# A state-space stage in another order, with its rotation inside two PSUM banks, and a rotary exchange by DMA copies instead of matmuls

## The chip, the core and the metric

One program on one core of a Trainium2 chip. The metric is the device time of one execution in microseconds (us). Four engines compute: TensorE (PE), VectorE (DVE), ScalarE (ACT) and GpSimd (POOL). SyncE (SP) only issues DMAs. Each engine works through its own queue in order, and semaphores carry the dependences between the queues. Matmuls write to eight banks of PSUM (2 KB per partition each); everything else is in SBUF. POOL and DMAs reach SBUF only.

## What is computed

Four layers on 512 tokens with 1024 channels, in fp32: a state-space and a latent-attention layer, each with a feed-forward, and two closing layers with three kinds of attention. The change touches the scan of the first layer and the partial rotary embedding of the closing ones:

```python
def s5_mixer(h, w_in, lam_re, lam_im, log_step, b_re, b_im, c_re, c_im, d_skip, w_glu):
    u = (h @ w_in).reshape(bsz, seq, 64, 16)             # 64 groups of 16 channels, 64 states each
    step = exp(log_step); decay = exp(lr * step)
    a = decay * (cos(li * step) + i sin(li * step))
    b = f(a, lr, li) * (b_re + i b_im)
    x[l] = a * x[l - 1] + b @ u[l]                        # complex, by an associative scan
    y = real(c @ x) + d_skip * u
    z = gelu(y)
    val, gate = split(z @ w_glu); return val * sigmoid(gate)

def _partial_rope(t, cos, sin):                           # closing layers, heads of 64, 16 dims turned
    x1, x2 = t[..., :8], t[..., 8:16]
    r1 = x1 * cos - x2 * sin
    r2 = x2 * cos + x1 * sin
    return concatenate([r1, r2, t[..., 16:]])
```

## The kernel before

**Products.** A product (L1827) is one tile of 128 output channels by 512 tokens: for each of eight slices of 128 input channels three matmuls, high x high, high x low and low x high (wh and wl, xH and xL), so that 24 float32r matmuls give fp32 accuracy. A weight block of 512 KB is loaded by SP into one of four raw buffers; ScalarE copies it to wh (split_high, L579), VectorE subtracts to get wl (split_low, L1093). Both run two blocks ahead of TensorE (ahead), and there are two buffers of wh and wl, so the copy for block n+2 starts when product n ends.

**Front of the state-space stage.** SP loads x, w_in and the parameters. ScalarE makes xH and the squares (two buffers, freed by TensorE through sq_used), VectorE makes xL. Product 0 of w_in is interleaved with the sum of squares, a plain fp32 matmul with ones of two passes for each slice, in bank 7 (L1969 to L1976). VectorE makes, between its xL steps, the powers of a (denominator, input_gain, powers, gained). From the sum ScalarE makes R, the inverse norm. VectorE multiplies each product by R into T (L1282), SP writes it to u_dram and reads it back in another layout (read_u: eight DMAs a quarter, U). POOL makes the rotation tables Er and Ei (E) and, in make_v, the output tables V (VM); VectorE makes the input tables G (make_g, five operations on 1024 columns) and the last part of Ei (last_phases).

**Four quarters.** The 64 groups go through in four quarters q of 16 groups. TensorE: states(q) (L1901) makes the chunk inputs z in banks 1 and 2; from_g (L1875) transposes G, which ScalarE copies to WM; lags (L1886) makes the short-range kernel; turn_z (L1932) turns the finished z back; outputs(q) applies the short-range kernel MS (Toeplitz, L1914) and then the states through V (L1922), into banks 6 and 3, and raises y_ready. VectorE, in each quarter: turn z by E (six operations with the temporaries rotr, roti, rott), zL of the quarter before, two scans (L1334), turn back (six operations into state), s_ready, make_g(q+2), lag0(q+1). lag0 adds the skip term to the lag row and puts it in MS; SP then spreads it by seven copies inside SBUF (mat_shift), after it has waited for the outputs and issued the reads of the next quarter. ScalarE does gelu (zs), WM, zH, the lag weights C2 and rho, the decay rows. Then comes the product with w_glu.

The queues are written out by hand. states(q+1) waits for z_read, given when VectorE has read both banks for the last time, and stands in TensorE's queue behind outputs(q).

**Closing layers.** For each layer eight tiles of q and k are projected (stage qk). ScalarE copies tile n from its bank to qk. rotate(n) on TensorE multiplies that tile with the constant permutation "rotate" into bank 4 or 5: an fp32 matmul of two passes, placed behind product n+1 (rotate(7) in the stage of v). VectorE's rope(n) then does bank x sin, tile x cos and their sum (L1683 to L1685), after the weight split of its turn. Afterwards POOL fills cq_exact and ck_exact by sixteen small DMAs (L561).

## Time and profile before

| | us |
|---|---|
| median of 3 runs | 1966.43 |
| lowest, highest | 1961.60, 1966.61 |
| the profiled execution | 1966.65 |
| its span in the trace | 1964.9 |
| TensorE busy in it | 1858.9 |
| VectorE, ScalarE, POOL busy | 1069.4, 832.9, 130.7 |

All stretches and rows are of the profiled execution; times count from the start of its span. A row of a timeline gives the start, the duration, the engine, the line of the kernel, the operation with what it writes and reads, and in brackets how long the engine had been idle before and who ended that. x with a number merges consecutive instructions. PEclk, in a stretch, is the granted clock of TensorE as a share of 2.4 GHz; 0.50 is 1.2 GHz. Matmuls overlap, so the distance of their starts is their cost, and their printed duration is longer.

### The profile page before, as it was taken

The numbers are of one execution on the slowest core, as the hardware profiler recorded it, in microseconds if no ns is written. First come the engines' busy times: TensorE is split into PE (matmuls) and PEld (weight loads), VectorE is DVE, ScalarE is ACT, GpSimd is POOL, SyncE is SP. The second block draws the span as 40 slices with busy tenths as digits, with TensorE's granted clock in tenths as the row PEclk, the third lists the DMA queues.
The fourth block names the chain that finished last, engine by engine and source line by source line (L and its number), as shares of the span: only waits on it lengthen the run. The fifth ranks groups of instructions, "written<-read, shape, count | busy, mean of one in ns | idle before, by whom it ended". The sixth has DMA issues, their size and how long they took to land.

```text
span 1964.9 us, 24248 instructions
## 1 busy us (share of the span) xinstructions
PE 1858.9 (95%) x8948; PEld 1432.2 (73%) x8948; DVE 1069.4 (54%) x1640; ACT 832.9 (42%) x1393; POOL 130.7 (7%) x164
## 2 busy tenths in 40 slices
PE   6787999999999879989999999989999999999997
PEld 3686778888888656657888888857766776866675
...
DMA packets 56828, 151.18 MB, mean 77 GB/s; under 512 B 15745, under 2 KB 20641, under 8 KB 56737
## 3 DMA queue, kind: packets, MB, share of 16 engines
...
## 4 chain that ended last, share of the span: by engine, by line
PE 84%; DVE 10%; ACT 4%; issue 1%; DMA 0%; POOL 0%; DVEq 0%; SPq 0%; ACTq 0%
PE bank L1836 18%; PE bank L1837 17%; PE bank L1838 17%; PE bank L2320 3%; PE bank L2322 3%; PE bank L2321 3%; PE bank L2297 2%; PE bank L2283 1%; PE bank L2282 1%; PE bank L2281 1%; PE bank L2041 1%; DVE wl L1096 1%; DVE G L1136 1%; PE bank L2069 1%; PE bank L2406 1%
## 5 line engine op out<-in xcount | busy, mean ns | idle before, releaser
L1096 DVE TENSOR_TENSOR wl<-raw,wh 128x1024 fp32r<-128x1024 f32 (+3 forms) x280 | 324.1, 1158 | 533.5 <-ACT wh L583 531.0
L583 ACT ACTIVATE wh<-raw 128x1024 fp32r<-128x1024 f32 (+3 forms) x280 | 279.0, 996 | 597.9 <-PE bank L1838 524.0
L1836 PE MATMUL bank<-xH,wh 128*128 128x512 f32 x896 | 359.5, 401 | 11.3 <-DVE wl L1096 9.4
L1837 PE MATMUL bank<-xL,wh 128*128 128x512 f32 x896 | 351.5, 392 | 0.0
L1838 PE MATMUL bank<-xH,wl 128*128 128x512 f32 x896 | 351.5, 392 | 0.0
L1836 PEld LDWEIGHTS bank<-xH,wh 128*128 128x128 f32 x896 | 170.2, 190 | 53.6 <-issue 15.3
L1837 PEld LDWEIGHTS bank<-xL,wh 128*128 128x128 f32 x896 | 170.1, 190 | 38.9 <-issue 4.1
L1838 PEld LDWEIGHTS bank<-xH,wl 128*128 128x128 f32 x896 | 169.8, 190 | 35.9
L1836 PE MATMUL bank<-hidH,wh 128*128 128x512 f32 x352 | 137.3, 390 | 0.0
L1838 PE MATMUL bank<-hidH,wl 128*128 128x512 f32 x352 | 136.9, 389 | 0.0
L1837 PE MATMUL bank<-hidL,wh 128*128 128x512 f32 x352 | 136.9, 389 | 0.0
L2320 PE MATMUL bank<-xH,wh 128*128 128x512 f32 x256 | 108.4, 423 | 0.0
L2322 PE MATMUL bank<-xH,wl 128*128 128x512 f32 x256 | 100.8, 394 | 0.0
L2321 PE MATMUL bank<-xL,wh 128*128 128x512 f32 x256 | 100.4, 392 | 0.0
L1736 DVE TENSOR_REDUCE least<-bank 128x1 f32<-128x128 f32 (+3 forms) x96 | 42.6, 485 | 73.8 <-PE bank L2304 73.7
L952 ACT ACTIVATE Pm<-bank,least 128x128 f32<-128x128 f32 (+3 forms) x96 | 49.9, 525 | 68.5 <-DVE least L1736 68.4
L1837 PEld LDWEIGHTS bank<-hidL,wh 128*128 128x128 f32 x352 | 66.1, 188 | 14.0 <-issue 0.2
L1838 PEld LDWEIGHTS bank<-hidH,wl 128*128 128x128 f32 x352 | 66.1, 188 | 13.8
L1836 PEld LDWEIGHTS bank<-hidH,wh 128*128 128x128 f32 x352 | 66.1, 188 | 13.8 <-issue 0.2
L720 ACT ACTIVATE hidH<-T 128x512 f32 (+1 forms) x44 | 27.8, 632 | 78.7 <-DVEq L1382 78.7
...
L2322 PEld LDWEIGHTS bank<-xH,wl 128*128 128x128 f32 x256 | 48.0, 188 | 11.0
...
## 6 DMA issues: line engine op xcount, KB each, us to landing
...
```

The source lines that it names most:

```text
L583: nc.scalar.activation(wh[:, (st.base + u) % 2, 0:kts * P], raw[:, (st.base + u) % 4, 0:kts * P], ACT.Copy).then_inc(w_high, 1)
L720: nc.scalar.activation(hidH[:, bass.ds(2 * i + u // 2, 1), :].rearrange("p o n -> p (o n)"), T[:, 3, :], ACT.Copy).then_inc(sem("hid_high" ...
L952: nc.scalar.activation(Pm[side][:, POFF[j]:POFF[j] + w], banks[side][:, 0:w], ACT.Exp, scale=-1.0, bias=least[:, j, side:side + 1], accum_ ...
L1096: nc.vector.tensor_tensor(wl[:, s, 0:kts * P], raw[:, (st.base + u) % 4, 0:kts * P], wh[:, s, 0:kts * P].bitcast(F32), ALU.subtract).then_ ...
L1736: nc.vector.tensor_reduce(least[:, j, side:side + 1], banks[side][:, 0:(j + 1) * P], AX, ALU.min)\
L1836: nc.tensor.matmul(bank, wh[:, s, w], hi[:, k, :], start=first and kt == 0, stop=False)
L1837: nc.tensor.matmul(bank, wh[:, s, w], lo[:, k, :], start=False, stop=False)
L1838: ins = nc.tensor.matmul(bank, wl[:, s, w], hi[:, k, :], start=False, stop=last and kt == kts - 1)
L2297: nc.tensor.matmul(banks[side][:, 0:w], qk[half_of(side), m, j * P:w], qk[half_of(side), 8 + m, 0:w], start=True, stop=False)
L2320: nc.tensor.matmul(bank, wh[:, s, w], xH[:, kt, :], start=kt == 0, stop=False)
L2321: nc.tensor.matmul(bank, wh[:, s, w], xL[:, kt, :], start=False, stop=False)
L2322: ins = nc.tensor.matmul(bank, wl[:, s, w], xH[:, kt, :], start=False, stop=kt == KD - 1)
```

## The change

- VectorE's front: all xL steps first, then the tables, then the inputs, with weight splits (next_block) and make_g put between them by hand. The squares have eight buffers (x_square: T, sq, acc, sd) and are summed behind product 1 with the constant ones. Products use the banks of in_bank. The w_in blocks and the constants are loaded ahead of B and C. The four conversions of constants move to the down projection of the first feed-forward.
- from_g(0), lags(0) stand behind product 4; states(0) ahead of product 7. from_g comes in two halves.
- The skip term is a matmul with skip_rows ahead of the lags; ScalarE copies the sum to MS (copy_lags). lag0 is gone.
- The rotation is in place in banks 1 and 2: every operation has one operand in a bank, rott and rotu are gone. states(q+1) waits for s_ready(q) instead of z_read, and stands ahead of the state outputs of q (state_outputs). V has a second and a third buffer (VM1, VM3), and POOL makes V(1) and V(3) without a wait for outputs; the E tables come first, V behind sd_ready.
- The rotary exchange: rotate and its constant are gone. POOL issues, for each tile, four copies of eight rows from qk to acc or sq, and rope(n) reads those. 

Core of the diff, without sizes and renamed names:

```diff
+    VM1 = [zL_mem.tensor("VM1r", [P, QP, P]), zH_mem.tensor("VM1i", [P, QP, P])]
+    VM3 = [T[:, 2:4, :].rearrange("p a (b c) -> p (a b) c", c=P), core.tensor("VM3i", [P, QP, P])]
+    skip_rows = zH_mem.tensor("skip_rows", [GK, NG, GK])
...
+    def exchanged(n):
+        return sq[:, 1, :] if n % 2 else acc[:, :]
...
+            load(stages["w_in"], 0, 1)
+            sp.dma_start(cons[:, :], con[:, 0:CON["cosA"][0]]).then_inc(sem("con_loaded"), 16)
+            load(stages["w_in"], 0, 2)
             sp.dma_start(Bz[:, 0:2, :, :].rearrange("p a b c -> p (a b c)"), ssm_b).then_inc(sem("b_loaded"), 16)
-            load(stages["w_in"], 0, 1)
             sp.dma_start(Cz[:, 0:2, :, :].rearrange("p a b c -> p (a b c)"), ssm_c).then_inc(sem("c_loaded"), 16)
-            sp.dma_start(cons[:, :], con[:, 0:CON["lag0"][1]]).then_inc(sem("con_loaded"), 16)
-            sp.dma_start(skip[:, :], ssm_d).then_inc(sem("mix_loaded"), 16)
+            load(stages["w_in"], 0, 3)
+            sp.dma_start(skip_rows[:, :, :].rearrange("p a b -> p (a b)"), ssm_d).then_inc(sem("mix_loaded"), 16)
             sp.dma_start(lam_par[:, :], lam_in).then_inc(sem("mix_loaded"), 16)
             sp.dma_start(wbf[:, :, :].rearrange("p a b -> p (a b)"), w_bf).then_inc(sem("mix_loaded"), 16)
-            for u in range(2, 8):
+            for u in range(4, 8):
                 load(stages["w_in"], u // 4, u % 4)
...
             pool.wait_ge(sem("sq_used"), KD)
+            pool.wait_ge(sd_ready, 1)
             make_v(0)
...
-            for q in range(1, NQ):
-                make_v(q)
+            pool.sem_inc(sem("pool_tables"), 1)
+            make_v(1)
+            pool.wait_ge(sem("v_ready"), 2)
+            pool.wait_ge(sem("y_ready"), 1)
+            make_v(2)
+            pool.wait_ge(sem("v_ready"), 3)
+            pool.wait_ge(sem("u_written2"), 32)
+            pool.wait_ge(sem("u_written3"), 32)
+            make_v(3)
 
...
-                    pool.dma_start(to, con[:, CON[name][0]:CON[name][1]]).then_inc(sem("rope_loaded"), 16)
+                    pool.dma_start(to, con[:, CON[name][0]:CON[name][1]]).then_inc(sem("rope_rows1"), 16)
+                for n in range(8):
+                    slot = n if n < 4 else n + 4
+                    pool.wait_ge(evicted, tiles[f"qk{layer}"] + n + 5)
+                    if n >= 2:
+                        pool.wait_ge(sem("roped"), 8 * layer + n - 1)
+                    elif n == 1:
+                        pool.wait_ge(sem("rope_rows1"), 288 * layer + 32)
+                    for at, source in ((0, 8), (8, 0), (HEAD, HEAD + 8), (HEAD + 8, HEAD)):
+                        pool.dma_start(exchanged(n)[at:at + 8, :], qk[source:source + 8, slot, :]).then_inc(sem(f"rope_rows{n % 2}"), 16)
...
+            split_high(stages["w_in"], 0, 1)
+
+            def x_squares(ks):
+                for k in ks:
+                    nc.scalar.activation(x_square(k), xT[:, k, :], ACT.Square).then_inc(sq_ready, 1)
+
...
+            x_squares(range(4))
+            next_block(0)
+            x_squares(range(4, KD))
+            next_block(1)
+            nc.scalar.preload_act_table_set("natural_log_exp_and_others")
+            act.wait_ge(sem("sq_used"), KD)
+            inverse_root(R[:, :], banks[7][:, :], 1.0 / D, sd_ready)
+            act.wait_ge(sem("powers_ready"), 1)
+            act.wait_ge(sd_ready, 1)
+            nc.scalar.activation(banks[7][:, :].rearrange("p (r l q) -> p r l q", r=2, l=CH), pf[:, 0:2, :, :], ACT.Copy)\
+              .then_inc(sem("pf_copied"), 1)
+            next_block(2)
+            act.wait_ge(sem("pool_tables"), 1)
+            lag_weights(0)
+            next_block(3)
+            next_block(4)
+            copy_w(0, (0, 1))
+            copy_w(0, (2, 3))
+            next_block(5)
+            lag_weights(1)
+            next_block(6)
+            next_block(7)
+            copy_w(1, (0, 1))
...
+            copy_lags(0)
+            copy_w(1, (2, 3))
             act.wait_ge(sem("phases_ready"), 1)
             decay_rows(0)
+            decay_rows(1)
             for q in range(NQ):
-                if q + 1 < NQ:
-                    lag_weights(q + 1)
-                    copy_w(q + 1)
-                    decay_rows(q + 1)
+                if q and q + 1 < NQ:
+                    copy_w(q + 1, (0, 1))
                 if q:
                     turned_high(q - 1)
+                if q and q + 1 < NQ:
+                    copy_w(q + 1, (2, 3))
+                    decay_rows(q + 1)
+                if q + 2 < NQ:
+                    lag_weights(q + 2)
+                if q + 1 < NQ:
+                    copy_lags(q + 1)
                 act.wait_ge(sem("y_ready"), q + 1)
...
+            for k in range(KD):
+                x_low(k)
+                if k == 1:
+                    split_low(st, 0, 0)
+            split_low(st, 0, 1)
+            denominator()
+            input_gain()
+            powers(1)
+            powers(2)
+            next_block(0)
+            powers(4)
+            gained()
+            next_block(1)
+            input_sums()
...
+            dve.wait_ge(sd_ready, 1)
+            take_input(0)
+            take_input(1)
+            next_block(2)
+            make_g(0, (0,))
+            take_input(2)
+            next_block(3)
+            make_g(0, (1,))
+            take_input(3)
+            next_block(4)
+            take_input(4)
+            last_phases()
+            take_input(5)
+            next_block(5)
+            make_g(1)
+            take_input(6)
+            next_block(6)
+            take_input(7)
 
             def turned_low(q):
                 for t in range(2):
...
                 tt(rotr[:, :, :], zr, er, ALU.mult)
-                tt(rott[:, :, :], zi, ei, ALU.mult)
-                tt(rotr[:, :, :], rotr[:, :, :], rott[:, :, :], ALU.add)
                 tt(roti[:, :, :], zi, er, ALU.mult)
-                tt(rott[:, :, :], zr, ei, ALU.mult)
-                dve.sem_inc(sem("z_read"), 1)
-                tt(roti[:, :, :], roti[:, :, :], rott[:, :, :], ALU.subtract)
+                tt(zr, zr, ei, ALU.mult)
+                tt(zi, zi, ei, ALU.mult)
+                tt(zi, rotr[:, :, :], zi, ALU.add)
+                tt(zr, roti[:, :, :], zr, ALU.subtract)
                 if q:
                     turned_low(q - 1)
                 dve.wait_ge(sem("rho_ready"), q + 1)
-                for r in (rotr, roti):
-                    step(nc.vector.tensor_tensor_scan(r[:, :, :].rearrange(flat), rho[:, q % 2, :, :].rearrange(flat),
-                                                      r[:, :, :].rearrange(flat), 0.0, ALU.mult, ALU.add))
+                re, im = zi, zr
+                for r in (re, im):
+                    step(nc.vector.tensor_tensor_scan(r.rearrange(flat), rho[:, q % 2, :, :].rearrange(flat),
+                                                      r.rearrange(flat), 0.0, ALU.mult, ALU.add))
+                tt(rotr[:, :, :], re, er, ALU.mult)
+                tt(roti[:, :, :], im, er, ALU.mult)
+                tt(re, re, ei, ALU.mult)
+                tt(im, im, ei, ALU.mult)
                 if q:
                     dve.wait_ge(sem("y_ready"), q)
-                for ri, (e0, e1, op) in enumerate(((er, ei, ALU.subtract), (ei, er, ALU.add))):
-                    tt(rott[:, :, :], rotr[:, :, :], e0, ALU.mult)
-                    tt(rotu[:, :, :], roti[:, :, :], e1, ALU.mult)
-                    tt(state[:, ri, :, 1:NCH], rott[:, :, 0:NCH - 1], rotu[:, :, 0:NCH - 1], op)
+                tt(state[:, 0, :, 1:NCH], rotr[:, :, 0:NCH - 1], im[:, :, 0:NCH - 1], ALU.subtract)
+                tt(state[:, 1, :, 1:NCH], roti[:, :, 0:NCH - 1], re[:, :, 0:NCH - 1], ALU.add)
                 dve.sem_inc(sem("s_ready"), 1)
+                if q == 0:
+                    next_block(KD - 1)
                 if q + 2 < NQ:
                     make_g(q + 2)
-                if q + 1 < NQ:
-                    lag0(q + 1)
             turned_low(NQ - 1)
 
...
-                    dve.wait_ge(sem("rotated"), 8 * layer + n + 1)
-                    step(nc.vector.tensor_tensor(sd[:, :], banks[4 + n % 2][:, :], rope_sin, ALU.mult))
+                    dve.wait_ge(sem(f"rope_rows{n % 2}"), (288 * layer + 32 if n % 2 else 256 * layer) + 64 * (n // 2 + 1))
...
+                nc.tensor.matmul(lag_bank(q)[:, 0:QG * GK], const("ident")[0:GK, :],
+                                 skip_rows[:, q * QG:(q + 1) * QG, :].rearrange("p g k -> p (g k)"), start=True, stop=False, skip_group_check=True)
...
-                    pe.wait_ge(sem("z_read"), q)
+                    pe.wait_ge(sem("s_ready"), q)
                 else:
-                    pe.wait_ge(evicted, tiles["w_glu"] + 4)
+                    pe.wait_ge(evicted, KD + 2)
...
+            from_g(1, (0, 1))
+            lags(1)
+            from_g(1, (2, 3))
+            outputs(0)
+            states(1)
+            state_outputs(0)
+            for q in range(1, NQ):
                 if q + 1 < NQ:
-                    from_g(q + 1)
-                if q:
-                    turn_z(q - 1)
+                    from_g(q + 1, (0, 1))
+                turn_z(q - 1)
                 if q + 1 < NQ:
+                    from_g(q + 1, (2, 3))
                     lags(q + 1)
                 else:
-                    pe.wait_ge(sem("z_read"), NQ)
+                    pe.wait_ge(sem("lag_ready"), NQ)
+                    pe.wait_ge(sem("w_ready"), 4 * NQ)
                     for u in range(2):
                         glu_part(u, range(KD - 4))
                 outputs(q)
+                if q + 1 < NQ:
+                    states(q + 1)
+                state_outputs(q)
...
-                def rotate(n):
-                    pe.wait_ge(evicted, tiles[f"qk{layer}"] + n + 5)
-                    if n >= 2:
-                        pe.wait_ge(sem("roped"), 8 * layer + n - 1)
-                    nc.tensor.matmul(banks[4 + n % 2][:, :], const("rotate"), qk[:, n if n < 4 else n + 4, :], start=True, stop=True)\
-                      .then_inc(sem("rotated"), 1)
```

VectorE at the start of the program (xT x, pw and pf powers of a, sm small factors). Before:

```order
L1102 SCALAR_TENSOR_TENSOR xL<-xT,vecs,xH 128x512 [waits dve_steps,high_ready,vecs_loaded]
L1102 SCALAR_TENSOR_TENSOR xL<-xT,vecs,xH 128x512 [waits high_ready]
L1096 TENSOR_TENSOR wl<-raw,wh 128x1024 [waits w_high]
L1136 TENSOR_TENSOR sm<-par 128x32
L1136 TENSOR_TENSOR sm<-par 128x32 [waits dve_steps]
L1136 TENSOR_TENSOR sm<-sm 128x32 [waits dve_steps]
L1168 RECIPROCAL sm<-sm 128x32 [waits dve_steps]
L1102 SCALAR_TENSOR_TENSOR xL<-xT,vecs,xH 128x512 [waits high_ready,dve_steps]
L1136 TENSOR_TENSOR pw<-sm 128x32 [waits factors_ready]
L1136 TENSOR_TENSOR pw<-sm 128x32 [waits dve_steps]
```

After:

```order
L1321 SCALAR_TENSOR_TENSOR xL<-xT,vecs,xH 128x512 [waits high_ready,vecs_loaded]
L1321 SCALAR_TENSOR_TENSOR xL<-xT,vecs,xH 128x512 [waits high_ready]
L1159 TENSOR_TENSOR wl<-raw,wh 128x1024 [waits w_high]
L1321 SCALAR_TENSOR_TENSOR xL<-xT,vecs,xH 128x512 [waits high_ready] x6
L1159 TENSOR_TENSOR wl<-raw,wh 128x1024 [waits w_high]
L1199 TENSOR_TENSOR sm<-par 128x32
L1199 TENSOR_TENSOR sm<-par 128x32 [waits dve_steps]
L1199 TENSOR_TENSOR sm<-sm 128x32 [waits dve_steps]
L1231 RECIPROCAL sm<-sm 128x32 [waits dve_steps]
L1199 TENSOR_TENSOR pw<-sm 128x32 [waits factors_ready,dve_steps]
```

The six xL steps, which stood one by one between tables, now come in one row ahead of the second weight split and of every table.

TensorE at the end of the third quarter's round (C lag weights, MS short-range kernel, VM the table V). Before:

```order
L1932 MATMUL bank<-cons,zs 64x64 [waits z_ready]
L1932 MATMUL bank<-cons,zs 64x64 x15
L1886 MATMUL bank<-C_86,G 128x32 [waits c_ready,lag_ready]
L1886 MATMUL bank<-C_86,G 128x32 x15
L1914 MATMUL bank<-MS,U_82 64x128 [waits shifted,h_ready]
L1914 MATMUL bank<-MS,U_82 64x128 x15
L1922 MATMUL bank<-VM,state 64x128 [waits s_ready,v_ready]
L1922 MATMUL bank<-VM,state 64x128 x31
L1901 MATMUL bank<-U_95,WM 64x64 [waits z_read,u_loaded1,w_ready]
L1901 MATMUL bank<-U_95,WM 64x64 x31
```

After:

```order
L1954 MATMUL bank<-skip_rows,cons 128x256 [waits c_ready,lag_ready]
L1959 MATMUL bank<-C_85,G 128x32 x16
L1990 MATMUL bank<-MS,U_81 64x128 [waits shifted,h_ready]
L1990 MATMUL bank<-MS,U_81 64x128 x15
L1975 MATMUL bank<-U_96,WM 64x64 [waits s_ready,u_loaded1,w_ready]
L1975 MATMUL bank<-U_96,WM 64x64 x31
L2001 MATMUL bank<-VM,state 64x128 [waits s_ready,v_ready]
L2001 MATMUL bank<-VM,state 64x128 x31
L2011 MATMUL bank<-cons,zs 64x64 [waits z_ready]
L2011 MATMUL bank<-cons,zs 64x64 x15
```

The states of the next quarter (U, WM) now come ahead of the state outputs (VM, state), a skip matmul has come in ahead of the lags, and the turning of z is followed by other work.

The rotary exchange. Before, on TensorE between the second and the third product of the projection:

```order
L1837 MATMUL bank<-xL,wh 128x512
L1838 MATMUL bank<-xH,wl 128x512
L2239 MATMUL bank<-qk,cons 128x512 [waits evicted]
L1836 MATMUL bank<-xH,wh 128x512 [waits w_split,evicted]
L1837 MATMUL bank<-xL,wh 128x512
```

After, on POOL, the first four tiles:

```order
L577 DMA rope_cos<-con_dram 128x512 [waits ln_delta]
L577 DMA rope_sin<-con_dram 128x512
L586 DMA acc<-qk 8x512 [waits evicted]
L586 DMA acc<-qk 8x512 x3
L586 DMA sq<-qk 8x512 [waits rope_rows1,evicted]
L586 DMA sq<-qk 8x512 x3
L586 DMA acc<-qk 8x512 [waits roped,evicted]
L586 DMA acc<-qk 8x512 x3
L586 DMA sq<-qk 8x512 [waits roped,evicted]
L586 DMA sq<-qk 8x512 x3
```

One matmul a tile (two passes on the chip) leaves TensorE's queue; four DMAs a tile come into POOL's, with a wait for the tile's eviction and, from the third tile on, for the rope step two tiles back.

## Rows read from the trace of the kernel before

**Rows 1.** The page, first part: engine, busy us (share of the span) x instructions.

```profile
PE 1858.9 (95%) x8948; PEld 1432.2 (73%) x8948; DVE 1069.4 (54%) x1640; ACT 832.9 (42%) x1393; POOL 130.7 (7%) x164
```

**Rows 2.** Stretch 120:140; busy of PE, PEld, DVE, ACT, POOL; clock, DMA share, GB/s.

```profile
120.00:140.00 20.00, 14.65 (x176) 13.86 (x178) 19.10 (x20) 3.33 (x7) 8.76 (x4) 0.68 0.16 39
```

**Rows 3.** Timeline of VectorE, front: start, us, engine, line, operation, [idle before <-releaser].

```profile
48.75 0.69 DVE L1282 TENSOR_TENSOR T<-bank,R 128x512 f32<-128x512 f32 x1 [3.33 <-PE bank L1838]
...
54.19 0.69 DVE L1282 TENSOR_TENSOR T<-bank,R 128x512 f32<-128x512 f32 x1 [3.06 <-PE bank L1838]
...
89.88 0.69 DVE L1282 TENSOR_TENSOR T<-bank,R 128x512 f32<-128x512 f32 x1 [4.27 <-PE bank L1838]
```

**Rows 4.** Timeline of TensorE, front of the state-space stage.

```profile
12.13 0.77 PE L1969 MATMUL bank<-xH,wh 128*128 128x512 f32 x1 [12.13 <-DVE wl L1096]
...
34.06 0.50 PE L1969 MATMUL bank<-xH,wh 128*128 128x512 f32 x1 [2.91 <-DVE xL L1102]
...
69.73 0.76 PE L1836 MATMUL bank<-xH,wh 128*128 128x512 f32 x1 [4.70 <-DVE wl L1096]
...
78.96 3.66 PE L1886 MATMUL bank<-C,G 128*128 128x32 f32 x32
...
98.48 3.77 PE L1875 MATMUL bank<-cons,G 128*128 128x128 f32 x16 [5.60 <-DVEq L1238]
...
102.04 6.88 PE L1886 MATMUL bank<-C,G 128*128 128x32 f32 x32
```

**Rows 5.** Timeline of VectorE, the four quarters.

```profile
104.08 1.23 DVE L1334 TENSOR_TENSOR_SCAN rotr<-rho,rotr 128x512 f32<-128x512 f32 x1
...
121.54 2.81 DVE L1136 TENSOR_TENSOR rotr<-rotr,rott 128x512 f32<-128x512 f32 x1
...
168.63 0.69 DVE L1136 TENSOR_TENSOR rotr<-bank,Er 128x512 f32<-128x512 f32 x1 [6.95 <-PE bank L1901]
...
194.97 0.69 DVE L1311 TENSOR_TENSOR zL<-bank,zH 128x512 fp32r<-128x512 f32 x1 [10.33 <-ACT zH L677]
```

**Rows 6.** Timeline of TensorE, the four quarters.

```profile
135.88 6.20 PE L1922 MATMUL bank<-VM,state 64*64 64x128 f32 x64 [4.04 <-DVEq L1342]
...
142.01 2.13 PE L1901 MATMUL bank<-U,WM 128*64 128x64 f32 x64
...
153.31 3.68 PE L1914 MATMUL bank<-MS,U 128*64 128x128 f32 x32 [0.27 <-DMA MS<-MS]
...
184.85 5.38 PE L1922 MATMUL bank<-VM,state 64*64 64x128 f32 x64 [4.25 <-DVEq L1342]
...
193.15 2.08 PE L1932 MATMUL bank<-cons,zs 64*64 64x64 f32 x64
```

**Rows 7.** Timeline of SP's queue, the quarters.

```profile
116.81 4.16 SPq L421 DMA_DIRECT2D U<-u_dram  x8
...
121.01 5.25 SPq L429 DMA_DIRECT2D MS<-MS  x7
...
142.11 3.99 SPq L421 DMA_DIRECT2D U<-u_dram  x8
```

**Rows 8.** Timelines of TensorE, ScalarE and VectorE, projections of the first closing layer.

```profile
1310.47 1.02 PE L2239 MATMUL bank<-qk,cons 128*128 128x512 f32 x2
...
1316.82 1.02 PE L2239 MATMUL bank<-qk,cons 128*128 128x512 f32 x2
...
1311.69 0.58 ACT L923 ACTIVATE qk<-bank 128x512 f32<-128x512 f32 x1
...
1312.96 0.68 DVE L1683 TENSOR_TENSOR sd<-bank,rope_sin 128x512 f32<-128x512 f32 x1
```

**Rows 9.** Timelines of POOL and VectorE there, and landing of the cq_exact copies.

```profile
1371.84 0.53 POOL L561 DMA_DIRECT2D cq_exact<-PT  x1 [0.29 <-POOL ck_exact L555]
...
DMA to landing us min/median/max: 1.5/2.4/3.5
...
1302.97 3.26 DVE L1670 TENSOR_SCALAR xT<-xT,vecs 128x512 f32<-128x512 f32 x8
```

238 lines of the change are left out of this document (97 added, 141 removed).

## The prediction

> **What bounds the kernel now.** I read the page's busy times first, then stretches of 20 us, then the timeline of each engine in the first 200 us and in the projections of a closing layer. TensorE is busy 95% of the span [rows 1]: elsewhere only work taken off TensorE counts, and a wait of another engine costs nothing. The exception is the state-space stage (0 to 200 us). From 120 to 140 us VectorE is busy 19.1 of 20 us and TensorE 14.7, at a granted clock of 0.68 [rows 2]: VectorE is the limit, and TensorE spends part of the time at the lower of its two levels (1.2 and 2.4 GHz). A product of 24 matmuls takes 5.44 us at the upper level (from one input taken to the next, 48.75 to 54.19 us [rows 3]).
>
> The front of the stage loses time in three places. The first product starts at 12.1 us, and its last step only at 34.1, behind a wait for xL: VectorE makes power tables between the xL steps. TensorE waits 4.7 us ahead of the seventh product, at 69.7 us [rows 4]. The eighth ends at 89.7 us [rows 3].
>
> **Part 1, the front.** Removed from the way of the first weight split are a square and a table load of ScalarE, some 2 us: the first product starts at 9.9 us. All xL steps stand ahead of the tables and the squares go to eight buffers instead of two, so it runs through: some 6.3 us at the lower level, as from 12.1 us before, and the rest at the upper one, 8.4 us together, to 18.3. Product 1 takes 5.4. The sixteen passes over the squares are of the kind of a rotation, whose two passes cost 0.91 us (part 4): 7.3. All this ends at 31 us. Before, it ended at about 43: **some 12 us earlier at this point.**
>
> Much of that is given back. VectorE now makes its tables in one piece, 21 us with two weight splits among them, and takes the first inputs at 36.6 us. G of the first quarter is ready at 52, with 2 us for meetings with POOL as in [rows 5]. The fifth product ends at 47.7, so TensorE waits 4.3 us: the 4.7 us wait of before is moved, not removed. Behind it now stand the 16 transposes and the lags, in small matmuls. In the trace that work took 3.8 and 6.9 us behind a wait of 5.6 us, the lags alone 3.7 without one [rows 4]. I take 10.7 us for both, the wait being nearly as long; without the low clock 5.8. Products 5, 6 and 7 and the states follow, 2 us longer for a cold start: the last product ends at 83 us, **6.5 earlier**; with a warm TensorE at 78, 11.5 earlier.
>
> From there to the first outputs: last input 84; through DRAM and back 6.6; seven shift copies issued 5.3 [rows 7] and landed 2.2 later, 98; Toeplitz product 3.7; states of the second quarter 2.1; state outputs 5.7: 109.7 us. Before it was 116.8 [rows 7]. The decay rows are now copied behind the transposes of G(1) on ScalarE, so the first scan waits for them to about 94.5, where its operands are ready at 88; its state is made at 101.4, still inside the chain. **First term: -7 us**; warm -10.5.
>
> **Part 2, the quarters.** VectorE does 14 operations a quarter on 512 columns (twelve of 0.69 us, two scans of 1.23 [rows 5]), five on 1024 for G at about 1.23, two zL and two for the lag row. An addition with both inputs in SBUF took 2.8 us where POOL was making V [rows 5]. TensorE makes the states of q+1 only after the state outputs of q, so the 16 us from states to s_ready (168.6 to 184.7) lie in series with 5.4 to 6.2 us of state outputs [rows 5, 6].
>
> Now the rotation works inside the two banks and holds them until s_ready, and each of its operations has one bank operand, none two SBUF ones. Reading a bank costs nothing: the product from a bank is 0.69 us like the rest [rows 5]. VectorE writing a bank is not in the trace. Nothing excludes a small gain; I take 0.03 us more each, between 0 and the 2.1 us that a blocked addition lost. The lag row goes to ScalarE and one small matmul. VectorE's quarter: 12 x 0.72 + 2 x 1.26 + 5 x 1.26 + 1.3 (zL) = 18.8 us, plus some 1.5 of waiting for zH: 20.3, where a quarter took 25.3 (116.8 to 142.1 [rows 7]) and 24.4 (to 166.5, the states' 2.1 us ahead of 168.6).
>
> What is late next: SP's queue. Behind the outputs it issues eight U reads (4.0 us) and then seven MS copies (5.3), and these land 2 us later. Before, the Toeplitz product of the next quarter started at 153.3, 11.2 us behind the outputs at 142.1, and its wait ended with that DMA [rows 6, 7]. This chain is unchanged. New pitch: 11.2 + 3.7 (Toeplitz) + 2.1 (states) + 5.7 (state outputs) = 22.7 us: **-2.6 and -1.7 us**. With TensorE at its upper level, Toeplitz at half and the state outputs at some 4 make 19.3, and VectorE's 20.3 decides: -9 together. V(3) follows V(2) at once now and meets G(3), which then takes 3 us longer, hidden under 22.7.
>
> From the third outputs to the fourth: gelu, and turning, zH and zL (the turn starts at 193.15, zL at 194.97 and ends 1.6 us later [rows 5, 6]) 5.4 us; scans 2.5; six operations 4.3; state outputs 5.4: 17.6 us. Before 23.7 (166.5 to 190.2 [rows 6]): **-6.1 us.**
>
> Stage: -7 - 2.6 - 1.7 - 6.1 = **-17.4 us**; warm -28.
>
> VectorE reads a bank and SBUF equally fast here, 0.69 us [rows 5]. The Trainium skill (VectorE: DVE Perf Modes, Rules for kernel authors) advises to copy a matmul's output out of PSUM first when many operations follow. By it two copies a quarter, 1.4 us, would pay for themselves; by the row they pay nothing.
>
> **Part 3, edits at nothing.** Four conversions of constants (1.8 us) leave the front for the down projection, where VectorE has slack behind TensorE's products; the constants are 64 KB shorter; the DMAs of w_in are issued ahead of B and C, both used only at 32 us and later. The skip rows' matmul, under 1 us a quarter, stands ahead of the shift wait, where TensorE has 1 to 2 us to spare; uncovered it would cost 4.
>
> **Part 4, rotary by DMA.** In the closing projections TensorE has no wait between products. Its pitch is 6.35 us (1310.47 to 1316.82 [rows 8]), a product is 5.44, so a rotation costs 0.91. Sixteen go: **-14.5 us**. In their place POOL issues four copies of 8 rows a tile: 0.5 us each, landed after 1.5 to 3.5 us, median 2.4 [rows 9]. These had 2 KB, the new ones 16 KB; I take the median. Together 2.0 + 2.4 = 4.4 us behind the eviction, at worst 5.5. The eviction ends 1.8 us behind its product (1312.3 against 1310.5), and VectorE takes the rotated tile 2.5 us behind the next product (1312.96 [rows 8]), that is 7.9 behind this one at the new pitch. Room: 6.1 us. If copies are late, VectorE waits with the next weight split queued behind; that has 2.9 us of its own (ready 2.5 us behind a product, needed at 5.4) before TensorE stands. So this cover fails from 9 us on.
>
> VectorE's eight additions of a constant, 0.41 us each, end about when the first copies are issued [rows 9]. The Trainium skill (SBUF — State Buffer, A bandwidth-pool intuition that's wrong) says that operations in this mode lock POOL out of writing descriptors, and tells of a POOL DMA stretched from 620 to 3100 ns. By it the first tile's copies would land 2.5 us later, an estimate: inside the room, and the sum is the same.
>
> **Sum.** 1966.65 us (the profiled execution; 1.75 lie outside its span of 1964.9) - 17.4 - 14.5 = 1934.8, rounded 1934.5. The median of the runs, 1966.43, is 0.2 from it.
>
> **Rivals.**
> A, *warm stage*: shorter waits keep TensorE at its upper level: 1966.65 - 28 - 14.5 = 1924. For it: the clock fell behind waits [rows 2, 4]. Against: small matmuls stayed at the lower level for 15 us.
> B, *the copies miss their tile*: they land over 8 us late and each tile waits as long as the rotation did: 1949. Against: 3.5 us was the worst seen.
> C, *the front gives all back*: tables in one row delay the last input to 89 us; stage -10, total 1942.
> D, *slower*: VectorE's eight bank writes a quarter. Each us more on one costs 8 us a quarter, 32 in all, less some 5 of slack in the two middle quarters. At the 2.1 us of a blocked addition: 1934.8 + 62 = 1997. It decides from 1.2 us a write. Nothing in the trace speaks for it.
> E, *nothing moves*: the rotation was hidden and the stage is held by something else: 1966. Against: TensorE without waits at 1310 us, VectorE full at 120.
>
> **How the numbers follow.** Forecast (1929 to 1940) 0.50, A 0.22, C 0.15, B 0.08, E 0.03, D 0.02. The range, 1919 to 1946, holds the first three but for A's end, and leaves out B, D and E. About 0.3%, 5.9 us, is what a measurement of this kernel can tell from no change. Faster (A, B, C, forecast) 0.95, same (E) 0.03, slower (D) 0.02.
>
> **What would show it.** Right: first matmul near 10 us, no wait in product 0, last product done at 78 to 84; outputs at about 110, 132, 155 and 173 us; Toeplitz waiting for MS copies; additions of 0.7 us beside POOL; a pitch of 5.44 us in the projections, with no wait of VectorE for acc or sq. Wrong: a pitch over 6, bank operations over 0.8 us, or TensorE's waits in the stage as long as before.

## The result

| | before | changed |
|---|---|---|
| median, us | 1964.01 | 1931.60 |
| lowest, highest | 1959.96, 1966.61 | 1929.83, 1933.28 |
| the profiled execution | 1966.65 | 1932.70 |
| its span in the trace | 1964.9 | 1930.8 |
| product with w_glu starts (third block), us in the span | 200.2 | 178.7 |

The ratio is 0.9824, 95% interval 0.9810 to 0.9837: 1.8% faster, 32.4 us between the medians and 34.0 between the two profiled executions. The forecast was 1934.5 in a range of 1919 to 1946. By stages the 34.0 us are 21.4 in the state-space stage, 14.4 in the closing layers, and 1.8 given back between. The 21.4 holds some variation of the kernel before: in another trace in which that stage runs the same instructions (the run with the rotary exchange alone, below) the third block started at 195.6 us instead of 200.2. Against that trace the stage gained 16.9 us.

**The front.** The first rows are of TensorE's timeline in the changed kernel (start, duration, line, what it writes and reads, idle time before and who ended it), and answer to [rows 3, 4].

```profile
9.52 0.80 PE L1903 MATMUL bank<-xH,wh 128*128 128x512 f32 x1 [9.52 <-DVE wl L1159]
...
23.43 3.59 PE L2044 MATMUL bank<-T,cons 128*128 128x512 f32 x8
...
47.41 1.09 PE L1942 MATMUL bank<-cons,G 128*128 128x128 f32 x8 [0.62 <-DVEq L1304]
...
49.05 3.76 PE L1959 MATMUL bank<-C,G 128*128 128x32 f32 x32
...
53.68 0.78 PE L1903 MATMUL bank<-xH,wh 128*128 128x512 f32 x1
54.25 0.63 PE L1904 MATMUL bank<-xL,wh 128*128 128x512 f32 x1
```

The first product starts at 9.5 us and runs without a wait; the squares are summed by 29.9; ahead of the transposes of G TensorE stands 0.6 us, where I had forecast 4.3. The lags take 3.76 us, the rate of the upper clock level. The clock still falls behind these small matmuls: the next product's matmuls follow each other at steps of 0.43 us (54.25, 54.68, 55.11), the lower level.

From 58 to 104 us the chain of waits (start, duration, engine and what it writes, line; only its pieces in this stretch) reads:

```profile
64.61 3.25 POOL Er L545
...
80.15 3.22 POOL VM L505
...
83.78 1.81 POOL MS L555
85.67 0.39 ACT MS L679
...
87.32 6.96 PE bank L1959 x32
94.29 1.77 PE bank L1942 x8
96.08 0.60 ACT WM L671
96.68 0.52 ACT rho L695
...
97.30 1.24 DVE bank L1394
```

This is not the chain that I forecast (last input, DRAM, shift copies). GpSimd makes the last table Er, then V, and only then clears MS, at 83.78. ScalarE's copy of the lag row into MS waits for that, TensorE's skip rows and lags for the copy, and the second half of the transposes behind them for the lags; behind their copy in ScalarE's queue stand the decay rows (rho), and the first scan starts at 97.30. TensorE's rows behind the wait:

```profile
86.11 1.22 PE L1954 MATMUL bank<-skip_rows,cons 16*128 16x256 f32 x2 [5.83 <-ACT MS L679]
87.25 7.04 PE L1959 MATMUL bank<-C,G 128*128 128x32 f32 x32
...
104.34 3.69 PE L1975 MATMUL bank<-U,WM 128*64 128x64 f32 x64 [5.60 <-DVEq L1404]
```

And a stretch in which they run (us, busy us of PE, PEld, DVE, ACT and POOL with their instructions, PEclk, DMA share, GB/s):

```profile
86.00:90.00 4.00, 3.90 (x15) 3.25 (x16) 0.41 (x1) 0.05 (x1) 3.84 (x3) 0.50 0.47 103
```

The lags behind the wait of 5.8 us take 7.04 us, at a granted clock of 0.50, 1.2 GHz. The late scan shows at 104.34: TensorE waits 5.6 us for the first state, and the states of the second quarter behind the wait take 3.7 us, where they took 2.1 in the kernel before [rows 6].

**The quarters.** SyncE's DMA queue (SPq), ScalarE and TensorE, in order of time; these answer to [rows 6, 7].

```profile
111.71 4.74 SPq L440 DMA_DIRECT2D U<-u_dram  x8
...
111.72 1.09 ACT L754 ACTIVATE zs<-bank 128x512 f32<-128x512 f32 x2 [11.18 <-PE bank L2001]
...
116.50 4.35 SPq L448 DMA_DIRECT2D MS<-MS  x7
...
122.61 3.68 PE L1990 MATMUL bank<-MS,U 128*64 128x128 f32 x32 [2.39 <-DMA MS<-MS]
...
132.88 1.09 ACT L754 ACTIVATE zs<-bank 128x512 f32<-128x512 f32 x2 [6.11 <-PE bank L2001]
...
154.03 1.09 ACT L754 ACTIVATE zs<-bank 128x512 f32<-128x512 f32 x2 [5.54 <-PE bank L2001]
...
168.82 1.09 ACT L754 ACTIVATE zs<-bank 128x512 f32<-128x512 f32 x2 [11.42 <-PE bank L2001]
```

The outputs come at 111.7, 132.9, 154.0 and 168.8 us (each gelu starts with them); before 116.8, 142.1, 166.5 and 190.2. Behind the outputs SyncE issues reads for 4.74 us and shift copies for 4.35, and the Toeplitz product starts 10.9 us behind the outputs, its wait ended by the copies. That is the chain of the prediction. VectorE's rotation in the banks, with GpSimd (POOL) at work on V beside it, from the timelines of both:

```profile
119.91 0.69 DVE L1199 TENSOR_TENSOR rotr<-bank,Er 128x512 f32<-128x512 f32 x1
...
120.58 2.35 POOL L505 TENSOR_TENSOR VM<-VM,tp 128x1024 f32<-128x1024 f32 x1
...
121.36 1.43 DVE L1199 TENSOR_TENSOR bank<-bank,Ei 128x512 f32<-128x512 f32 x2
122.83 0.68 DVE L1199 TENSOR_TENSOR state<-rotr,bank 128x504 f32<-128x504 f32 x1
...
127.40 1.67 DVE L1199 TENSOR_TENSOR G<-tv,G 128x1024 f32<-128x1024 f32 x1
...
128.07 3.22 POOL L503 TENSOR_TENSOR T<-tp,T 128x1024 f32<-128x1024 f32 x1
...
130.36 2.01 DVE L1199 TENSOR_TENSOR G<-G,tv 128x1024 f32<-128x1024 f32 x1
```

Writing a bank takes 0.71 us an operation (1.43 for two), against 0.69 for writing SBUF; beside GpSimd none of the twelve is stretched. G, with both inputs in SBUF at 127.40 and 130.36, is: 1.67 and 2.01 us for 1.22.

**The rotary exchange.** The timelines of ScalarE, whose weight copies follow the products, of GpSimd and of VectorE, in a stage of q and k; they answer to [rows 8, 9].

```profile
1298.44 1.99 POOL L586 DMA_DIRECT2D acc<-qk  x4 [3.46 <-ACT qk L986]
...
1302.05 1.06 ACT L617 ACTIVATE wh<-raw 128x1024 fp32r<-128x1024 f32 x1 [3.90 <-PE bank L1905]
...
1303.21 1.22 DVE L1159 TENSOR_TENSOR wl<-raw,wh 128x1024 fp32r<-128x1024 f32 x1 [2.16 <-ACT wh L617]
1304.36 0.68 DVE L1750 TENSOR_TENSOR sd<-acc,rope_sin 128x512 f32<-128x512 f32 x1
...
1307.49 1.06 ACT L617 ACTIVATE wh<-raw 128x1024 fp32r<-128x1024 f32 x1 [3.90 <-PE bank L1905]
```

The pitch is 5.44 us (1302.05 to 1307.49). Four copies take 2.0 us to issue; over all 64 the time from issue to landing was 1.7 to 3.9 us, median 3.2. VectorE takes the exchanged rows at 1304.36 straight behind its split, without a wait.

### The profile page after: what moved, and what is told of

Its sections match the earlier page's. It is cut to its first block, busy times and chain, and to the rows that moved or that the text cites. A ratio compares the mean times of both kernels' runs of the same rounds, so it can differ in the third digit from the quotient of the medians.

```text
span 1930.8 us, 24262 instructions
## 1 busy us (share of the span) xinstructions
PE 1839.9 (95%) x8924; PEld 1422.0 (74%) x8924; DVE 1054.1 (55%) x1631; ACT 834.1 (43%) x1397; POOL 167.7 (9%) x228
## 4 chain that ended last, share of the span: by engine, by line
PE 84%; DVE 5%; ACT 4%; POOL 4%; issue 2%; SPq 1%; DMA 0%; ACTq 0%; DVEq 0%; POOLq 0%
PE bank L1903 17%; PE bank L1905 17%; PE bank L1904 17%; PE bank L2390 3%; PE bank L2392 3%; PE bank L2391 3%; PE bank L2367 2%; PE bank L2354 2%; PE bank L2355 2%; PE bank L2353 2%; PE bank L2123 1%; DVE wl L1159 1%; PE bank L2151 1%; PE bank L2477 1%; PE bank L2405 1%
## 5 line engine op out<-in xcount | busy, mean ns | idle before, releaser
L1903 PEld LDWEIGHTS bank<-hidH,wh 128*128 128x128 f32 x352 | 66.1, 188 | 13.9 <-issue 0.2
L1905 PEld LDWEIGHTS bank<-hidH,wl 128*128 128x128 f32 x352 | 66.1, 188 | 13.7
```

The source lines that it names most:

```text
L1903: nc.tensor.matmul(bank, wh[:, s, w], hi[:, k, :], start=first and kt == 0, stop=False)
L1905: ins = nc.tensor.matmul(bank, wl[:, s, w], hi[:, k, :], start=False, stop=last and kt == kts - 1)
```

## Experiments

Each was timed in four executions beside runs of the kernel before on the same chip; ratios are to the kernel before. Differences in us to the changed kernel are between medians of different rounds, in which the kernel before itself had medians of 1964.0 to 1966.2; differences of 1 to 3 us therefore rest on the traces alone. "Third block" is the start of the third block of w_glu on TensorE, which ends the stage (200.2 us before, 178.7 changed).

### The rotary exchange alone

Edit, on the kernel before:

```diff
+                    for at, source in ((0, 8), (8, 0), (HEAD, HEAD + 8), (HEAD + 8, HEAD)):
+                        pool.dma_start(exchanged(n)[at:at + 8, :], qk[source:source + 8, slot, :]).then_inc(sem(f"rope_rows{n % 2}"), 16)
...
-                    nc.tensor.matmul(banks[4 + n % 2][:, :], const("rotate"), qk[:, n if n < 4 else n + 4, :], start=True, stop=True)\
-                      .then_inc(sem("rotated"), 1)
```

> The kernel before with the rotary exchange by copies and nothing else. Theory (the rotations stood on TensorE's path and the copies are hidden): the pitch of the q and k products falls from 6.35 to 5.44 us, 16 rotations of 0.91 us go, 14.5 us together: about 1951 us, a ratio of 0.9926; VectorE waits for no copy. Rival (the exchange was or is hidden behind something else): the pitch stays over 6 us and the time at 1964 to 1966.

Measured: 1950.7 us, ratio 0.9931 (0.9909 to 0.9953). Between the start of the closing layers and the end the trace gains 13.9 us. The term of the rotary exchange stands. Two more things stand in this trace, in a stage that the edit doesn't touch. Its third block starts at 195.6 us, 4.6 sooner than in the profiled execution of before: so much does that stage vary of itself. And around 700 us of its span, in the latent attention, it loses 2.2 us; the changed kernel loses 1.5 us there (below).

### How much cover the copies have

Edit, on the changed kernel (two parts; the other run has three, of 176, 168 and 168 columns; the counts that the waits for these copies ask for change with it):

```diff
-                        pool.dma_start(exchanged(n)[at:at + 8, :], qk[source:source + 8, slot, :]).then_inc(sem(f"rope_rows{n % 2}"), 16)
+                      for c in (slice(0, 256), slice(256, 512)):
+                        pool.dma_start(exchanged(n)[at:at + 8, c], qk[source:source + 8, slot, c]).then_inc(sem(f"rope_rows{n % 2}"), 16)
...
```

> The changed kernel with each exchange copy cut into two of half the columns: 8 copies a tile, 4.0 us to issue, and 3.2 to land: 7.2 us behind the eviction, against a room of 6.1. Theory (VectorE gets the tile 1 us late, but TensorE only stands from 9 us on): a pitch of 5.44 us and the time of the changed kernel, 1932. Rival (there is no second cover): 1.1 us a tile more, 15 us, 1947.

> The changed kernel with each exchange copy cut into three parts: 12 copies a tile, 6.0 us of GpSimd's time to issue, more than the 5.44 of a product. Theory (the cover fails about here: 6.0 + 3.2 = 9.2 us behind the eviction against the 9 at which TensorE stands): the pitch goes to GpSimd's 6.0 us, 0.5 us for each of 14 tiles, 7 to 9 us slower than the changed kernel: 1939 to 1941. Rival (the copies are not on any path even then): 1932. Second rival (each us past the room of 6.1 is paid, as the two-part run denied): 3.1 us a tile, 1975.

Measured: 1933.7 us with two parts (0.9834, 0.9818 to 0.9851), which can't be told from the changed kernel, and 1948.6 with three (0.9908, 0.9892 to 0.9925), 17 us slower than it, twice what I expected. The halves landed sooner than the whole copies, in 2.4 us (median) instead of 3.2, so a tile's rows came some 6.4 us behind its eviction, and VectorE waited for them only twice, 0.7 and 2.6 us: this run hardly tested the room. The rows of the three-part run do, and show where its time went; the timelines of GpSimd, VectorE, ScalarE and TensorE together:

```profile
1320.07 0.69 DVE L1751 TENSOR_TENSOR sd<-acc,rope_sin 128x512 f32<-128x512 f32 x1 [3.91 <-DMA acc<-qk]
...
1323.39 5.92 POOL L587 DMA_DIRECT2D acc<-qk  x12
...
1332.08 0.69 DVE L1751 TENSOR_TENSOR sd<-acc,rope_sin 128x512 f32<-128x512 f32 x1 [3.90 <-DMA acc<-qk]
...
1334.26 0.74 DVE L1782 TENSOR_SCALAR T<-bank,vecs 4x512 f32<-4x512 f32 x1
...
1335.03 0.63 ACT L993 ACTIVATE T<-T 4x512 f32<-4x512 f32 x1 [7.54 <-DVE T L1782]
...
1337.96 1.22 DVE L1160 TENSOR_TENSOR wl<-raw,wh 128x1024 fp32r<-128x1024 f32 x1 [2.96 <-ACT wh L618]
...
1339.24 0.79 PE L2354 MATMUL bank<-wh,xH 128*128 128x512 f32 x1 [3.76 <-DVE wl L1160]
1339.83 0.63 PE L2355 MATMUL bank<-wl,xH 128*128 128x512 f32 x1
```

GpSimd issues without a pause, 5.91 us a tile. The exchanged rows of the tiles are there 7.3 to 11.3 us behind the end of their eviction, later from tile to tile; VectorE waits for them (3.9 us at 1320.07), but TensorE stands nowhere in this stage and the pitch of the products stays at 5.44. At the seventh tile VectorE waits 3.9 us for acc again. Behind that stands the bias row of the forget gate (1334.26), ScalarE has waited 7.5 us for it with its next weight copy queued behind, and the weight split comes at 1337.96. TensorE waits 3.8 us there, and starts again at the lower clock level (steps of 0.43 us until 1344, 2.4 us more). With what follows it is 6.5 us in the first closing layer and 8.9 in the second, all of it behind the stage. The expectation had the right cause, GpSimd's 6 us a tile, but the pitch that it priced it by did not move.

### The rotation through SBUF again

Edit, on the changed kernel:

```diff
                 tt(rotr[:, :, :], zr, er, ALU.mult)
+                tt(rott[:, :, :], zi, ei, ALU.mult)
+                tt(rotr[:, :, :], rotr[:, :, :], rott[:, :, :], ALU.add)
                 tt(roti[:, :, :], zi, er, ALU.mult)
-                tt(zr, zr, ei, ALU.mult)
-                tt(zi, zi, ei, ALU.mult)
-                tt(zi, rotr[:, :, :], zi, ALU.add)
-                tt(zr, roti[:, :, :], zr, ALU.subtract)
+                tt(rott[:, :, :], zr, ei, ALU.mult)
+                tt(roti[:, :, :], roti[:, :, :], rott[:, :, :], ALU.subtract)
...
-                re, im = zi, zr
-                for r in (re, im):
+                for r in (rotr[:, :, :], roti[:, :, :]):
...
-                tt(re, re, ei, ALU.mult)
-                tt(im, im, ei, ALU.mult)
...
+                for ri, (e0, e1, op) in enumerate(((er, ei, ALU.subtract), (ei, er, ALU.add))):
+                    tt(rott[:, :, :], rotr[:, :, :], e0, ALU.mult)
+                    tt(rotu[:, :, :], roti[:, :, :], e1, ALU.mult)
+                    tt(state[:, ri, :, 1:NCH], rott[:, :, 0:NCH - 1], rotu[:, :, 0:NCH - 1], op)
```

> The changed kernel with the rotation's intermediate results in two buffers of SBUF again; order and waits as in the changed kernel. Theory (an operation of VectorE with both inputs in SBUF is held up by GpSimd, one with an input in a bank isn't): the ten such operations of the second and third quarter that fall between 112 and 137 us, where GpSimd makes V, take about 2.0 us instead of 0.7, 13 us together; less 1.9 us of slack in each of two quarters, about 9 us slower than the changed kernel: 1941. Rival (only the order and the waits matter): the operations take 0.7 us and the time stays at 1932.

Measured: 1946.5 us (0.9903, 0.9882 to 0.9923), 14.9 slower than the changed kernel. VectorE's timeline in the second quarter, and at the start of the third:

```profile
114.64 0.69 DVE L1201 TENSOR_TENSOR roti<-bank,Er 128x512 f32<-128x512 f32 x1
...
120.39 2.85 DVE L1395 TENSOR_TENSOR_SCAN roti<-rho,roti 128x512 f32<-128x512 f32 x1
123.27 2.66 DVE L1201 TENSOR_TENSOR rott<-rotr,Er 128x512 f32<-128x512 f32 x1
125.97 2.38 DVE L1201 TENSOR_TENSOR rotu<-roti,Ei 128x512 f32<-128x512 f32 x1
...
146.66 0.69 DVE L1201 TENSOR_TENSOR rotr<-rotr,rott 128x512 f32<-128x512 f32 x1
150.77 1.21 DVE L1395 TENSOR_TENSOR_SCAN rotr<-rho,rotr 128x512 f32<-128x512 f32 x1
```

The operation with a bank as input takes 0.69 us beside GpSimd; the scans and the six operations with both inputs in SBUF take 2.1 to 2.9 us while GpSimd makes V(2) and V(3), and 0.69 and 1.21 when it is done (146.66, 150.77). The outputs of that quarter come 34.3 us behind the first instead of 21.2, and the others at the old distance. So what the banks give is not that the operations are shorter, but that none of them meets GpSimd. I had counted ten such operations, 13 us together, less two slacks of 1.9. They lost 14.4 us, all in one quarter, so that the slack came off once: the quarter is 13.1 us longer and the third block 13.7 later. These 15 us are the price of SBUF in the changed order, in which GpSimd makes V(2) and V(3) one behind the other. In the kernel before, where the rotation was in SBUF too, its additions and scans lost 3.1 to 3.5 us a quarter beside GpSimd; so the 15 us are not a share of the 34.

### The states behind the state outputs again

```diff
             outputs(0)
+            state_outputs(0)
             states(1)
-            state_outputs(0)
...
                 outputs(q)
+                state_outputs(q)
                 if q + 1 < NQ:
                     states(q + 1)
-                state_outputs(q)
```

> The changed kernel with the states of the next quarter behind the state outputs again; all else as changed. The prediction held that the 16 us from states to s_ready lay in series with the state outputs: by that each of three quarters grows by 3.7 us, +7 to +11, 1939 to 1943. Rival: VectorE has its G to make behind s_ready (124.4 to 132.4 us in the trace of the changed kernel) and would not take the states any sooner, while the outputs come 2.6 to 3 us sooner and with them SyncE's reads and shift copies: the pitch falls from 21.1 to VectorE's 20.3 to 20.7, 0 to 2 us faster: 1930 to 1932.

Measured: 1934.5 us (0.9840, 0.9819 to 0.9862), third block at 179.8: 1 us later in the trace, too little to be told from the changed kernel. The outputs come at 110.9, 130.1, 151.5 and 169.9 us. The first three come sooner, as the rival said: SyncE starts 0.9 and 2.8 us earlier, and VectorE has G to make anyway. The fourth comes 18.4 us behind the third instead of 14.8: there VectorE has no G left, and TensorE waits 3.0 us for s_ready ahead of the last state outputs. The prediction's reason for this part holds in the last quarter alone.

### The shift copies ahead of the reads

```diff
+            mat_shift(0)
             for q in range(NQ):
-                mat_shift(q)
+                if q + 1 < NQ:
+                    mat_shift(q + 1)
                 if q + 2 < NQ:
                     sp.wait_ge(sem("y_ready"), q + 1)
```

> The changed kernel with the seven shift copies of the next quarter issued ahead of the reads of U of the one after it, and so ahead of the wait for outputs. Theory (SyncE's queue of 11 us is what sets the pitch, with VectorE's 20.3 to 20.7 us close behind): the Toeplitz products lose their waits of 2.4 and 3.1 us, and the pitch falls from 21.1 to 20.3 to 20.7: 1 to 2 us faster in all, 1930. Rival (SyncE alone): the waits come off in full, 5.5 us, 1926. Second rival (VectorE sets it already): nothing.

Measured: 1930.3 us (0.9819, 0.9803 to 0.9835), third block at 176.5, 2.2 sooner. The 1.3 us between the medians can't be told from no change; what follows is read from the trace. The waits of Toeplitz for MS are gone; the outputs follow each other by 19.0 and 20.9 us instead of 21.2 and 21.2. SyncE's chain was the bound of the changed kernel, and VectorE stands 0 to 2 us behind it.

### The first quarter: G early, and MS cleared by ScalarE

```diff
             take_input(4)
-            last_phases()
+            make_g(1)
             take_input(5)
             next_block(5)
-            make_g(1)
+            last_phases()
```

> The changed kernel with G of the second quarter made while VectorE is idle (50.2 to 58.7 us) ahead of the last phases. TensorE's wait of 3.5 us at 74.8 us goes, and the last input is written about 5 us sooner (77 instead of 82). Theory (the first outputs hang on GpSimd: V, then the clearing of MS at 85.6 us, then the skip rows' matmul, the transposes of G and the decay rows): they stay near 111.7 us, 0 to 1.5 us faster, 1930 to 1932. Rival (they hang on the last input, as the prediction had it): 5 us faster, 1927.

Measured: 1931.2 us (0.9829, 0.9808 to 0.9849), third block 0.8 us sooner: no change that could be told. The wait of 3.5 us at 75 is gone, and the wait for MS has grown from 5.8 to 11.2 us. The last input does not decide.

```diff
-            step(nc.gpsimd.memset(rho[:, :, :, 0:1], 0.0))
-            step(nc.gpsimd.memset(state[:, :, :, 0:1], 0.0))
-            step(nc.gpsimd.memset(MS[:, :, :, :], 0.0))
-            pool.sem_inc(sem("pool_tables"), 1)
...
-            copy_w(1, (0, 1))
...
-            act.wait_ge(sem("pool_tables"), 2)
+            act.wait_ge(sem("u_ready"), KD)
+            act.wait_ge(sem("phases_ready"), 1)
+            for zero in (rho[:, :, :, 0:1].rearrange("p a b c -> p (a b c)"), state[:, :, :, 0:1].rearrange("p a b c -> p (a b c)")):
+                step(nc.scalar.activation(zero, sm[:, 0, 0:2 * QP], ACT.Copy, scale=0.0))
+            step(nc.scalar.activation(MS[:, 0:CH - 1, :, :].rearrange("p a b c -> p (a b c)"), Bz[:, :, :, :].rearrange("p a b c -> p (a b c)")[:, 0:(CH - 1) * QG * GK], ACT.Copy, scale=0.0))
+            decay_rows(0)
             copy_lags(0)
+            copy_w(1, (0, 1))
             copy_w(1, (2, 3))
-            act.wait_ge(sem("phases_ready"), 1)
-            decay_rows(0)
```

> The changed kernel with MS, and the first columns of state and rho, cleared by ScalarE behind the last input instead of by GpSimd behind V, and the decay rows copied at once. Theory (GpSimd's queue and the decay rows behind it set the first outputs): the skip rows' matmul loses its wait of 5.8 us, the first scan its wait of 10.9; the first state is ready at about 93 us instead of 104.1, then SyncE's chain from the last input decides (Toeplitz at 95.5): first outputs at about 104 instead of 111.7, 7 us faster, 1924 to 1926. Rival (something else holds the first outputs): 0 to 2 us.

Measured: 1922.8 us (0.9777, 0.9761 to 0.9794), 8.8 faster than the changed kernel, third block at 169.5. ScalarE's timeline in that run:

```profile
81.84 1.70 ACT L733 ACTIVATE MS<-Bz 128x1792 f32<-128x1792 f32 x1
83.57 0.62 ACT L691 ACTIVATE rho<-sm 128x504 f32<-128x504 f32 x1
84.10 0.37 ACT L675 ACTIVATE MS<-bank 128x256 f32<-128x256 f32 x1
...
102.37 1.09 ACT L753 ACTIVATE zs<-bank 128x512 f32<-128x512 f32 x2 [3.81 <-PE bank L2000]
```

The decay rows are there at 84.2 instead of 97.2, the first scan starts at 85.8 instead of 97.3, and the first outputs come at 102.4 instead of 111.7. But the edit does two things. It takes the clearing out of GpSimd's queue, and it moves the decay rows, in ScalarE's queue, ahead of the lag copy and of the copies behind the transposes. The rows tell them apart: the lag copy and what TensorE does behind it come only 1.6 us sooner (the copy at 84.10 for 85.67, the skip rows' matmul at 84.5 for 86.1, Toeplitz at 94.4 for 96.0), so no more than that comes from the clearing. The scan comes 11.5 us sooner; with it TensorE's wait of 5.6 us for the state goes, and the states take 2.1 us instead of 3.7. An estimate from these rows: 1.6 us of the 9.3 are the clearing's, the rest comes of the place of the decay rows. No run has either alone.

### All three, and further

> The changed kernel with all three edits: G of the second quarter early, MS cleared and the decay rows copied behind the last input, shift copies ahead of the reads of U. Theory: the last input at about 77 us, the first outputs at 97 to 100 instead of 111.7, the pitch at VectorE's 20.3 to 20.7: 12 to 16 us faster, 1916 to 1920. Rival (GpSimd's V of the first quarter, ready at 83 to 85, or the cold clock hold the first outputs): not over 8 us faster, 1924.

Measured: 1917.8 us (0.9753, 0.9737 to 0.9770), 13.8 faster than the changed kernel and 48 than the one before, the best version of this study. The outputs come at 99.8, 119.3, 139.8 and 154.6 us. The three edits alone gave 0.4, 1.3 and 8.8 us, 10.5 together, where the intervals are 1.5 to 2 us wide to either side. The early G seems to pay only beside the edit of MS and the decay rows: the first outputs come 2.6 us sooner than with that edit alone (99.8 for 102.4), and without it the early G brought them 0.7 (111.0 for 111.7).

Then three more edits on top: the lags of the second quarter don't wait for MS, `take_input(7)` stands ahead of the weight split, and the first shift copies ahead of the reads (first run) or on ScalarE's queue (second run). The first run's:

```diff
+                    if j == 7:
+                        mat_shift(0)
                     read_u(j // 7)
...
             take_input(6)
-            next_block(6)
             take_input(7)
...
                 if q == 0:
+                    next_block(6)
                     next_block(KD - 1)
...
-                if q:
+                if q >= 2:
                     pe.wait_ge(sem("lag_ready"), q)
```

> The kernel with the three edits, and further: the lags of the second quarter don't wait for MS (the bank they write is another), the last input is taken ahead of a weight split, and SyncE issues the first shift copies ahead of the reads of U. Theory (the way from the last product to the first outputs is last input, MS cleared, shift copies, Toeplitz): TensorE's wait of 5.7 us at 75 us goes, the last input comes 2 us sooner, the first outputs 3 to 6 us sooner than the 99.8 of the run with three edits: 1912 to 1915. Rival (GpSimd's V, ready at 83.4, or VectorE's first state at 89 decide): 0 to 2 us, 1916 to 1918.

> As the run before, but ScalarE issues the first seven shift copies itself, beside SyncE's reads of U. Theory: Toeplitz and U come at the same time, about 87 us, the first outputs 6 to 8 us sooner than 99.8: 1910 to 1912. Rival (VectorE's first state and its G of the third quarter, ready at 89 and 100, hold the second quarter): the same as the run before.

Measured: 1920.5 (0.9770, 0.9752 to 0.9788) and 1921.6 us (0.9776, 0.9759 to 0.9792), a little slower than with three edits, if anything. The first outputs did come sooner, at 96.0 and 94.2 us. The third outputs come at 142.1 us in the first of them, for 139.8. The time went here (first of the two runs, timelines of VectorE and TensorE):

```profile
85.40 5.40 DVE L1161 TENSOR_TENSOR wl<-raw,wh 128x1024 fp32r<-128x1024 f32 x2
...
100.13 1.97 PE L1944 MATMUL bank<-cons,G 128*128 128x128 f32 x8 [4.21 <-DVEq L1306]
102.03 3.68 PE L2013 MATMUL bank<-cons,zs 64*64 64x64 f32 x64
```

Two weight splits now stand behind the first state, both with inputs in SBUF, and GpSimd makes V(1) beside them: 5.4 us for 2.5. G of the third quarter is ready at 100.1, as before these edits (100.0), TensorE waits 4.2 us for it, and the transposes and the turn behind the wait run at the lower clock level (1.97 and 3.68 us for 1.09 and 2.08). The gain of 4 to 6 us became a wait and a slower spell behind it.

## Why the prediction was right, step by step

| term | forecast, us | measured |
|---|---|---|
| first outputs | -7.0 | -5.1 |
| first to second, second to third | -2.6, -1.7 | -4.1, -3.3 |
| third to fourth | -6.1 | -8.9 |
| state-space stage | -17.4 | -21.4 |
| rotary exchange | -14.5 | -14.4 |
| between them | 0 | +1.8 |
| all | -31.9 | -34.0 (-32.4 between the medians) |

Against the other trace of the stage before (outputs at 113.4, 137.7, 162.0 and 185.7) the first term is -1.6 instead of -5.1, and the steps between quarters are -3.2, -3.2 and -8.8. The 4.0 us by which the stage beat its forecast thus lie within what the stage of before varies by, and the first term may have been forecast far too large: that the sum came out so close is partly luck.

**The front.** The steps up to 31 us came as forecast (first product 9.5 for 9.9, squares 29.9 for 31). Two steps failed and offset each other, which is luck. "TensorE waits 4.3 us" for G was mis-sized: VectorE's tables took 18.3 us instead of 21, so that it took its first input at 33.3 instead of 36.6, and the wait was 0.6 us. The transposes and lags behind it took 6.3 us instead of 10.7, and the last product ended at 74.8, not at 83. And the step "the first scan waits for them to about 94.5 ..., still inside the chain" was wrong: I had put the decay rows behind the transposes of G(1), but not followed what stands ahead of those: the lag copy, which waits for the clearing of MS on GpSimd, and the lags, which ran at the lower level (7.0 us). The scan came at 97.3, the state was made at 104.1, and TensorE stood 5.6 us for it. The run with MS cleared by ScalarE shows what the two are worth together, 9 us; by its rows 1.6 of them are the clearing and the rest is the place of the decay rows.

**The quarters.** The mechanism, SyncE's chain, was right: 10.9 us for 11.2, and the run with the copies first removes it. Mis-sized was the term of the state outputs: 5.7 us, taken from rows behind waits of 4 us, became 3.7 at the upper level, while the states ahead of them took 3.1 and 2.5 instead of 2.1; 22.7 came out as 21.2. The same and a shorter way through gelu and zL (4.0 us for 5.4) make the last quarter 14.8 instead of 17.6. In that sense rival A, the warm stage, was half true: from 100 to 140 us the granted clock was 0.83, before 0.66 to 0.68. (Its 28 us are 1 more than its parts, 10.5, 9 and 7.5, add up to.)

**VectorE.** Bank writes cost 0.02 us each, 0.03 was forecast, and rival D is out. That an operation with a bank input doesn't meet GpSimd was in the prediction as a remark on the additions. It is the larger effect in the new order: 15 us when taken away there. In the kernel before, the same conflict cost VectorE only 3.1 to 3.5 us a quarter. With VectorE's quarter left at 20.3 by the prediction, the reason for it stood only in "none two SBUF ones". The Trainium skill (VectorE: DVE Perf Modes, Rules for kernel authors), which names copying out of PSUM first as the way when many operations follow, would have lost this: the trace disagrees for a kernel with GpSimd at work, 0.69 us from a bank against 2.1 to 2.9 from SBUF.

**The rotary exchange.** Pitch 5.44, no wait of VectorE for acc or sq, 14.3 us. The landing of 3.2 us (median) was above the 2.4 that I took; the slowest tiles used the room of 6.1 in full. "This cover fails from 9 us on" was not borne out. The three-part run had rows 9.6 to 11.3 us late and TensorE still had no wait between the products: I had left out that VectorE also stands idle 2.2 us ahead of its split, which makes the cover some 11.2 us, an estimate from the rows. What that run lost, it lost behind the stage, where the forecast had looked at nothing. Whether VectorE's additions hold up GpSimd's first copies, as the Trainium skill says (SBUF — State Buffer, A bandwidth-pool intuition that's wrong), no run here shows: the additions ended at 1286.6, 0.2 us before the first copy was issued.

**Between them.** 1.5 of the 1.8 us were lost around 680 us, which no term had. The row of the statistic there:

```profile
681.39 2.04 PE L2203 MATMUL bank<-T,means 128*128 128x512 f32 x2 [2.02 <-ACT R L642]
```

Two matmuls take 2.04 us, for 1.10 in the kernel before: the lower clock level. The run with the rotary exchange alone loses 2.2 us at this place, without the moved conversions, and the run with the shift copies first loses nothing here, with them (it loses 1.4 to 1.5 us around 880 us). So the conversions are not its cause; why the clock falls in one place or the other stays open.
